# Compressor's first layer with the weights held in TensorE, one gated sum moved on VectorE, and a split wait in the last down pair

## The reference

```python
for l in range(DEPTH):
    m = token_mixer(x, w_in[l], ...)
    x = layer_norm(ALPHA * x + m, ...)
    f = swiglu(x, ...) if l % 2 == 0 else moe_swiglu(x, ...)
    x = layer_norm(ALPHA * x + f, ...)

def nsa_compress(kv, pos, w1, b1, w2, b2):
    chunks = kv.reshape(b, t // 16, 16, g, dh)
    blocks = jnp.concatenate([chunks[:, :-1], chunks[:, 1:]], axis=2) + pos[:, None, :]
    flat = blocks.transpose(0, 1, 3, 2, 4).reshape(b, nc, g, 32 * dh)
    hid = jax.nn.gelu(flat @ w1 + b1)
    return hid @ w2 + b2

proj = jnp.einsum('btcw,cwd->btcd', ys, w_br)          # three branches
m = jnp.sum(sigmoid(mgate) * proj, axis=2) @ w_out
swiglu = (silu(x @ w_gate) * (x @ w_up)) @ w_down
```

## Time and profile before

| what | value |
|---|---|
| median of three runs | 1960.12 us (1959.55 to 1962.38) |
| the profiled execution's own time | 1961.21 us |
| its span in the trace | 1959.4 us |
| PE busy | 1880.9 us, 96% |
| weight loads of PE busy (PEld) | 1632.8 us, 83% |
| DVE busy | 1424.9 us, 73% |
| ACT busy | 1139.7 us, 58% |
| mean granted clock of PE | 0.984 |

### The profile page before, as it was taken

One profiled execution on the slowest core, in us unless ns is written; L12 is line 12 of the kernel. 1 busy time (PEld: TensorE's weight loads), 2 busy tenths in 40 slices (PEclk: granted clock), 3 DMA queues, 4 the chain that ended last, 5 costly groups with the idle time before them and its releaser, 6 DMA issues.

```text
span 1959.4 us, 27929 instructions
## 1 busy us (share of the span) xinstructions
PE 1880.9 (96%) x11075; PEld 1632.8 (83%) x11075; DVE 1424.9 (73%) x1197; ACT 1139.7 (58%) x965; POOL 0.2 (0%) x4
## 2 busy tenths in 40 slices
PE   7999998999989999997999999999999999999996
PEld 7999998999979999996887878878778788788784
DVE  4585566544465665667888878888888888888887
ACT  5444444343435444344777777777677677776774
POOL 0000000000000000000000000000000000000000
PEclk9999998999989999998999999999999999999999
DMA  8543444554535334453998989989989899898994
GB/s 321 183 162 129 154 170 157 194 187 174 201 132 217 136 140 149 164 183 135 365 362 306 362 334 342 361 307 366 369 300 363 328 349 362 310 363 335 341 362 173
DMA packets 36170, 506.78 MB, mean 259 GB/s; under 512 B 3984, under 2 KB 4112, under 8 KB 5264
## 3 DMA queue, kind: packets, MB, share of 16 engines
q1 hardware_dynamic: 35104, 500.16, 68.1%
q10 hardware_dynamic: 1008, 5.77, 0.8%
HBM read 504.86 MB, written 1.05 MB: 258 GB/s over the span
## 4 chain that ended last, share of the span: by engine, by line
PE 84%; DVE 6%; issue 4%; DMA 3%; ACT 2%; DVEq 0%; SPq 0%; ACTq 0%
PE PS L342 15%; PE PS L344 15%; PE PS L343 15%; PE PS L328 10%; PE PS L329 10%; PE PS L330 10%; DMA raw<-wstream 3%; DVE w_lo L1104 2%; PE PS L773 2%; DVE tmp L1551 2%; PE PS L733 2%; ACT w_hi L817 1%; PE PS L473 1%; PE PS L505 1%; PE PS L488 1%
## 5 line engine op out<-in xcount | busy, mean ns | idle before, releaser
L1104 DVE TENSOR_TENSOR w_lo<-raw,w_hi 128x2048 fp32r<-128x2048 f32 x473 | 1082.4, 2290 | 395.7 <-ACT w_hi L817 395.3
L817 ACT ACTIVATE w_hi<-raw 128x2048 fp32r<-128x2048 f32 x473 | 905.3, 1916 | 371.5 <-PE PS L344 263.5
L328 PE MATMUL PS<-xT_hi,w_hi 128*128 128x256 f32 x1456 | 423.7, 291 | 13.2 <-DVE w_lo L1104 6.0
L329 PE MATMUL PS<-xT_lo,w_hi 128*128 128x256 f32 x1456 | 416.7, 286 | 0.0
L330 PE MATMUL PS<-xT_hi,w_lo 128*128 128x256 f32 x1456 | 416.3, 286 | 0.0
L342 PE MATMUL PS<-w_hi,xT_hi 128*128 128x512 f32 x896 | 357.7, 399 | 1.5 <-DVE xT_lo L1541 1.5
L344 PE MATMUL PS<-w_hi,xT_lo 128*128 128x512 f32 x896 | 349.5, 390 | 0.0
L343 PE MATMUL PS<-w_lo,xT_hi 128*128 128x512 f32 x896 | 348.6, 389 | 0.0
L328 PEld LDWEIGHTS PS<-xT_hi,w_hi 128*128 128x128 f32 x1456 | 284.1, 195 | 24.6 <-issue 19.7
L329 PEld LDWEIGHTS PS<-xT_lo,w_hi 128*128 128x128 f32 x1456 | 284.3, 195 | 0.2
L330 PEld LDWEIGHTS PS<-xT_hi,w_lo 128*128 128x128 f32 x1456 | 284.1, 195 | 0.0
(11 more groups left out here) (241 smaller groups left out, 1352.4 us busy)
## 6 DMA issues: line engine op xcount, KB each, us to landing
raw<-wstream SPq DMA_DIRECT2D x237, 2048.0 KB, 8.0
soft<-ln ACTq DMA_DIRECT2D x4, 1024.0 KB, 6.3
X<-x SPq DMA_DIRECT2D x1, 1024.0 KB, 5.0
out<-X ACTq DMA_DIRECT2D x2, 512.0 KB, 2.7
cst<-consts SPq DMA_DIRECT2D x1, 890.5 KB, 10.9
sm<-small SPq DMA_DIRECT2D x1, 729.0 KB, 12.7
bufA<-router ACTq DMA_DIRECT2D x1, 512.0 KB, 3.5
rg<-constb SPq DMA_DIRECT2D x1, 335.0 KB, 11.4
```

The lines of the kernel that those rows point to most:

```text
L328: mm(o, wh, rhs_hi[:, k, :], start=(k == 0), stop=False)
L329: mm(o, wh, rhs_lo[:, k, :], start=False, stop=False)
L817: activate(w_hi[:, at % RING], raw_half(at // 2 % RING, at % 2), ACT.Copy).then_inc(hi_done, 1)
L1104: v.tensor_tensor(w_lo[:, at % RING], raw_half(at // 2 % RING, at % 2), w_hi[:, at % RING], ALU.subtract).then_inc(lo_done, 1)
```

## The change

It has three parts.

**1. The compressor's first layer.** Now a 128 x 128 block of weights is stationary and z moves. The high and the low part of z lie side by side in `act_hi`, so one matmul with `w_hi` moves both (2 x 34 strided columns, `ZN` = 34: 32 chunks, the position column and one more), and one with `w_lo` moves the high part alone (34 columns). A step has 8 x 2 x 2 = 32 matmuls, a layer 128. The sums come out with features on the partitions, in two PSUM banks. ACT's copy (L873) and PE's transposes (L424) are gone; DVE adds the two parts with two reductions into `hid` (SBUF), adds the bias in one instruction, and ACT's GELU reads `hid`.

**2. DVE's order at s = 34 and 35.** The first gated sum of step 35 is done in step 34, between `retained` and the split of sub-tile 37; the second stays in step 35; `retained_lower` moves from step 34 to the end of step 35.

**3. The last down pair.** For token tile 0, each of the two sub-tiles waits for its own half of the hidden features, where both halves were waited for before the first.

```diff
-ZM = 79
+ZN = 34
...
-        z_hi = act_hi[:, :, :].rearrange("p a t -> p (a t)")[:, 0:6 * P]
-        z_lo = act_lo[:, :, :].rearrange("p a t -> p (a t)")[:, 0:6 * P]
-        zg_hi, zg_lo = (z.rearrange("p (g m) -> p g m", g=6) for z in (z_hi, z_lo))
+        z = act_hi[:, :, :].rearrange("p a t -> p (a t)")[:, 0:12 * P].rearrange("p (h m) -> p h m", h=2)
+        zg_hi, zg_lo = (z[:, h, :].rearrange("p (g m) -> p g m", g=6) for h in range(2))
+        hid_ps = PS[:, YB:YB + 2, 0:4 * ZN].rearrange("p c (v h n) -> p c v h n", v=2, h=2)
...
-            def last_pair(s, lhs, outs, ks, cols):
+            def last_pair(s, lhs, outs, ks, cols, b=None):
 
                 for t in range(TT):
                     for n in range(2):
                         if t == 0:
                             sub_ready(s + n)
+                            if b is not None:
+                                pe.wait_ge(hT_rdy, 2 * b + n + 1)
...
-                    o = PS[0:ZM, YB, kv * CH:(kv + 1) * CH]
                     for j in range(8):
                         jj = 8 * half + j
-
-                        def z(a):
-                            return a[:, kv * P + jj:kv * P + jj + 8 * (ZM - 1) + 1:8]
-                        wh, wl = (w[:, slot, j * CH:(j + 1) * CH] for w in (w_hi, w_lo))
-                        mm(o, z(z_hi), wh, start=(jj == 0), stop=False)
-                        mm(o, z(z_hi), wl, start=False, stop=False)
-                        last = mm(o, z(z_lo), wh, start=False, stop=(jj == 15))
+                        first = 3 * kv * P + jj
+                        zs = z[:, :, first:first + 8 * (ZN - 1) + 1:8]
+                        for c in range(2):
+                            o = hid_ps[:, c, kv]
+                            at = slice(j * CH + c * P, j * CH + (c + 1) * P)
+                            mm(o, w_hi[:, slot, at], zs, start=(jj == 0), stop=False)
+                            last = mm(o[:, 0], w_lo[:, slot, at], zs[:, 0], start=False, stop=(jj == 15))
...
-                def hidden_to_features():
-                    pe.wait_ge(hid_rdy, l + 1)
-                    for n in range(4):
-                        last = nc.tensor.transpose(PS[:, MB, n * ZM:(n + 1) * ZM], hid[0:ZM, n * P:(n + 1) * P],
-                                                   ident[0:ZM, 0:ZM])
-                    last.then_inc(ht_ps, 1)
...
-                    elif s == 7:
-                        activate(hid[0:ZM, :], PS[0:ZM, YB, :], ACT.Copy).then_inc(hid_rdy, 1)
...
-                    dve.wait_ge(lo_done, base + s + RING)
+                    dve.wait_ge(lo_done, base + s + RING - (ms == (0,)))
...
-                        for m in range(2):
+                        for m in ms:
...
                 for s in range(MIX):
-                    after(s)
+                    after(s, (1,) if s == RET0 + 4 else (0, 1))
                     if s == 8:
-                        dve.wait_ge(ht_ps, l + 1)
+                        dve.wait_ge(sub_used, base + 8)
                         for kv in range(2):
-                            o = PS[:, MB, 2 * ZM * kv:2 * ZM * (kv + 1)].rearrange("p (c n) -> p c n", c=2)
-                            last = v.tensor_tensor(hbias[:, 2 * kv:2 * kv + 2], o[:, :, 32 * (kv + 1)],
-                                                   sm[:, l, S_B1 + 2 * kv:S_B1 + 2 * kv + 2], ALU.add)
+                            last = v.reduce_sum(hid[:, 2 * kv:2 * kv + 2, :],
+                                                hid_ps[:, :, kv].rearrange("p c h n -> p c n h"), AX_X)
+                        chain.link(last)
+                        last = v.tensor_tensor(hbias[:, :], hid[:, :, 32], sm[:, l, S_B1:S_B1 + 4], ALU.add)
                         last.then_inc(hbias_rdy, 1)
...
                     if s == RET0 + 3:
                         retained()
+                        after(s + 1, (0,))
...
-                    if s == RET0 + 3:
+                    if s == RET0 + 4:
                         retained_lower()
```

More of the change, by code:

```diff
@@ L156, in trunk @@
         tmp = sb("tmp", [P, 2, T])
-        hid = tmp[:, :, :].rearrange("p a t -> p (a t)")
+        hid = tmp[:, :, :].rearrange("p a t -> p (a t)")[:, 0:4 * ZN].rearrange("p (c n) -> p c n", c=4)
         hidT = sb("hidT", [P, 4, NG * NC])
@@ L237, in trunk @@
         z_hi_rdy, vt_ps, v_rdy = sem("z_hi_rdy"), sem("vt_ps"), sem("v_rdy")
-        hid_rdy, ht_ps, hbias_rdy, hidT_rdy, w2_ps, kc_rdy = (
-            sem(n) for n in ("hid_rdy", "ht_ps", "hbias_rdy", "hidT_rdy", "w2_ps", "kc_rdy"))
+        hbias_rdy, hidT_rdy, w2_ps, kc_rdy = (sem(n) for n in ("hbias_rdy", "hidT_rdy", "w2_ps", "kc_rdy"))
         s_ps, max_rdy, exp_rdy, prob_rdy, pt_ps, ptA_rdy, ptD_rdy, av_ps, yA_hi, yA_lo = (
@@ L591, in mixer @@
                 for s in range(MIX):
-                    if s == 9:
-                        hidden_to_features()
                     if s == 10:
@@ L649, in down @@
                     if final:
-                        pe.wait_ge(hT_rdy, 2 * b + 2)
-                        last_pair(s, lhs, outs, ((0, 1), (2, 3)), 1024)
+                        last_pair(s, lhs, outs, ((0, 1), (2, 3)), 1024, b)
                         return
@@ L848, in after @@
                     sub = OUT0 > s >= BRANCH0
-                    if not (s in (0, 1, 2, 3, 7, 9, 10, 11, 15, 20, 21, 22, 23) or sub):
+                    if not (s in (0, 1, 2, 3, 9, 10, 11, 15, 20, 21, 22, 23) or sub):
                         return
@@ L939, in after_hidden @@
                     for n in range(4):
-                        off = ZM * n + 32 * (n // 2)
                         last = activate(hidT[:, n, :].rearrange("p (g c) -> p g c", g=NG),
-                                        PS[:, MB, off:off + 32].rearrange("p (g c) -> p g c", g=NG)[:, :, 0:NC], ACT.Gelu_apprx_tanh,
+                                        hid[:, n, 0:32].rearrange("p (g c) -> p g c", g=NG)[:, :, 0:NC], ACT.Gelu_apprx_tanh,
                                         bias=hbias[:, n:n + 1])
@@ L1203, in gated, with after @@
                         chain.link(v.tensor_tensor(o, o, tmp[:, :, :], ALU.add))
-                def after(s):
+                def after(s, ms=(0, 1)):
                     if s >= OUT0:
```

## The result

| | before | changed |
|---|---|---|
| median, lowest to highest | 1959.84 us (1959.47 to 1962.38, four runs) | 1975.03 us (1970.43 to 1977.19, four runs) |
| span of the profiled execution | 1959.4 us | 1968.6 us |
| mean granted clock of PE | 0.984 | 0.975 |

The changed kernel is slower: ratio of the medians 1.0069, 95% interval 1.0057 to 1.0082. I had forecast 1950.1 us, and the slower time that I had worked out for a clock that falls in the compressor was 1972.5 us. That is the case that came.

A forecast was written before the change was run, and what follows sets the result against it. PE's own work and standstills were taken to bound the kernel. Gains of 2.2 + 4.4 + 3.0 + 0.4 = 10.0 us from 1961.2, less 1.1 to the median, gave 1950.1 us; own range 1946.5 to 1955, overall 1946.5 to 1974.5.

The forecast's parts named there:

- Part 3, 2.2 us: Last down pair: tile 0's first 12 matmuls cover the wait for the second half, DVE just free; gain 2.2 us.
- Part 2, 4.4 us: Steps 34 and 35: PE's 2.19 us stop for the gated product goes in both layers; gain 4.4 us.
- the clock's 3.0: Behind the two gated stops: the stretches at clock 0.50 go, 1.5 us each; gain 3.0 us.
- Part 1, pace of the loads: Compressor: loads set the pace, matmuls 0.112 us apart, 14.3 us a layer in place of 14.56.
- Part 1, the clock: Compressor: estimated at the full-clock pace throughout, gaining 0.4 us over two layers; a falling clock was left to a rival.
- The rival, 1972.5 us: Compressor: clock falls to 1.2 GHz, matmuls 0.213 us apart, stage and step 8 cost 22 us more; chance 0.36.
- Transposes and the copy, nothing: Steps 7 and 9: removal costed at nothing; PE waits 0.3 us longer for GELU, bias ready before the table load ends.

The follow-up runs named there:

- e3: The kernel before with only the split wait of the last down pair (part 3 alone): 1958.51 us, ratio 0.9984.
- e3b: The kernel before with only DVE's new order at steps 34 and 35 (part 2 alone): 1953.41 us, ratio 0.9964.
- e2: The kernel before with only the new compressor (part 1 alone): 1985.99 us, ratio 1.0129.
- e4: The changed kernel with both matmuls of a pair moving 2 x 62 strided columns of z: 1949.96 us, ratio 0.9943.
- e1: The kernel before with parts 2 and 3 and the old compressor: 1951.19 us, ratio 0.9954.
- e8: The changed kernel with both matmuls of a pair moving the 68 columns of both parts: 1969.75 us, ratio 1.0061.

## Why the prediction was wrong

- **Part 3, 2.2 us: right.** e3 gives 2.4, by the steps described: the wait covered by tile 0's first 12 matmuls, DVE only just free.
- **Part 2, 4.4 us and the clock's 3.0: right.** e3b gives 7.4. That the clock falls behind each stop was too firm, though: e2 has a stop without a fall, and is 1.5 us better off for it.
- **Part 1, pace of the loads: right at the full clock.** Starts 0.11 us apart, and 14.26 us a layer in e4 against the 14.3 forecast. The formula of the Trainium skill ("TensorE: Matmul & The Clock Gate", LDWEIGHTS), a load's columns / 1.2 ns, had given an estimate of 13.7 us for the stage; e4's 14.26 is above it.
- **Part 1, the clock: this is the step that failed.** The forecast took the compressor at clock 1.00 from end to end, on the ground that loads and matmuls follow each other without a break, and put the stage at 0.4 us less for both layers. The stage has no break, and the clock fell in it in both layers: part 1 alone costs 25.1 us (e2), 22.0 of them in the two compressors and the two steps 8. What it misjudged was which rows resemble the stage: the stretch of short matmuls at 63.41, behind which the clock fell, was set aside for its 1 us of standing still. e4 shows that the columns that PE moves made the difference here: same loads, same records of 100% busy, more columns, clock kept.
- **The rival, 1972.5 us: right in kind, 2.5 us short.** Its 22 us for the stage and step 8 are the 22.0 of e2's rows, though when the clock falls was a guess: it let it fall 3.6 us into the stage, and the changed kernel has 5.96 and 2.78. Part 1 costs 25.1: 0.9 more is PE's wait for GELU. The other 2 us stand in e2's trace behind the second layer of the compressor, where DVE's splits fall back by 1.0 us more in layer 0 (80.26 to 117.11, before 68.62 to 104.47) and 1.2 in layer 1 (655.75 to 691.70, before 633.69 to 668.44). e2 runs there at 0.50 for 6.83 and 3.42 us, the kernel before for 3.41 us in layer 0 alone. Traces with the old compressor differ at this place too (e1 has none in layer 0), so it isn't shown that part 1 makes it.
- **Transposes and the copy, nothing: nearly.** The timeline of ACT, DVE and PE at that place in the changed kernel:

```profile
71.40 1.28 ACT L928 ACT_TABLE_LOAD   x1
72.70 0.95 ACT L928 ACTIVATE hidT<-tmp,hbias 128x30 f32<-128x30 f32 x4
...
72.15 0.16 DVE L1378 TENSOR_TENSOR hbias<-tmp,sm 128x4 f32<-128x4 f32 x1
...
73.79 0.60 PE L426 MATMUL PS<-hidT,sm 128*128 128x30 f32 x4 [1.48 <-ACT hidT L928]
```

The bias is done at 72.31, before the table load ends at 72.68, as forecast. PE waits 0.43 us longer than before, not 0.3: GELU takes 0.95 us for its four instructions where it took 0.81 in the trace of before. It reads SBUF now and not PSUM; whether that is the reason was not tried.

The clock-gate part of the Trainium skill ("TensorE: Matmul & The Clock Gate") says that an engine which isn't busy is throttled to 1.2 GHz. Here 1.2 GHz was granted for 20.48 and 27.30 us in which PE's records are 100% busy, so those records don't tell which stage that rule takes for idle.

## What to carry to other kernels

Before a matmul's operands are swapped so that few columns move, ask what the stage still moves: a stage that mostly loads weights can lose TensorE's clock, and then its loads come 0.21 us apart in place of 0.11. Read the granted clock of the stage first and the busy share after it; the busy share was 100% here in the run that lost and in the run that won. If a strided stationary operand is what limits a stage, write it so that its columns adjoin before exchanging the operands (11.21 us in place of 14.56).

## What the runs showed that I had not expected

- **The clock falls under a fully busy PE.** 27.30 us at 1.2 GHz with PE and its loads busy throughout, 68 and 34 columns moving; e8 with 68 and 68 also falls; e4 with 124 and 124 keeps 2.4 GHz. Doing more arithmetic in the same instructions made the kernel faster.
- **Loads slow with the clock.** 128 columns are 0.11 us apart at 2.4 GHz and 0.21 us at 1.2 GHz, though only 34 or 68 columns move; the records go from 192 to 333 ns.
- **Stride costs a stationary operand; for a moving one no cost shows.** 79 stationary columns at a stride of 8: 248 ns, adjoining: 148 ns. 124 moving columns at the same stride fit within the 0.11 us of a load, where a smaller cost could hide. The Trainium skill ("SBUF — State Buffer", the paragraph on cachelines) says that each access that crosses to a new 16-byte line pays a penalty. The load times agree with it; e4 shows none for the moving columns.
